# Scaling attention probabilities ahead of the next maxima, and a last output tile by halves, in a one-core decoder layer

## Chip, cores and metric

The kernel runs on one core of a Trainium2 chip. The metric is device time in microseconds of one execution, taken as the median of several runs. All numbers are float32 on the way in and out.

## What is computed

One layer of a hybrid decoder for 1024 prompt rows and 8 x 8 sample rows: an input projection, sliding-window attention with sinks and a relative bias, a pooling mixer, gates, and a squared-ReLU MLP between RMS norms. The two parts that matter here are the softmax of the attention and the last lines of the layer:

```python
s = einsum(q, k) * HEAD_DIM ** -0.5 + bias
m = maximum(max(s, axis=-1), sink)
p = exp(s - m)
denom = sum(p, axis=-1) + exp(sink - m)
o = einsum((p / denom), v)
...
f = square(relu(rms_norm(h, g_pre_mlp) @ w_mlp_up)) @ w_mlp_down
return h + rms_norm(f, g_post_mlp)
```

## The kernel before

Each engine runs its own list of instructions in order, and semaphores tie the lists together. Every product is made of three TensorE products, of high and low parts of both operands (`products`, `row_products`); ScalarE writes the high part of a result and VectorE the low part.

**Attention.** The work is cut into 17 units: 16 of the prompt (two blocks of 128 queries of two heads each; a unit has four score tiles `x`) and one for all sample rows. All engines walk through the same steps `s` (`for s in range(A_STEPS)`), and in step `s` each does a piece of several units, together with one filler: a third of one tile of the input projection (24 products of 384 or 320 columns), which keeps TensorE working between attention pieces.

- TensorE in step `s`: scores of unit `s` (`score_products`, L1344 to L1346), filler group `s + 1` (L1232 to L1234), values of unit `s - 2` (`weigh_values`, L1386, L1390), and the turning (transposing) of the probabilities of unit `s - 1` (`turn_probs`, L1251), which waits for `p_norm`.
- VectorE in step `s`: maxima of unit `s` (four score tiles plus bias into `pr`, L957, and the statistics L967 to L969, which release `stats`); then the scaling of unit `s - 1`: sum of the exponentials (L973), reciprocal (L974), a fold of the two halves of the window (L978), and four multiplications (L983), the last of which releases `p_norm`; then the filler's low part (L891), in every third step the low part of the next weights (L845), the low part of the output of unit `s - 2` (L993), and the masked second copy `pt` of the turned probabilities of unit `s - 1` (L1004).
- ScalarE in step `s`: exponentials of unit `s` (L636, L640), which wait for `stats`; the filler's copy (L580 or L573); every third step the high part of the next weights (L543); the high part of the output of unit `s - 2` (L653); and the first copy `pt` of the turned probabilities of unit `s - 1` (L660).
- GpSimd does the pooling (L469 to L498) from the time the first pooling columns come out of the fillers, around unit 8.

The order on VectorE, where `u` is set twice per step, is

```python
u = s
...
dve.tensor_scalar(stat[:, NM, u % 4, :], ...).then_inc(stats, 1)
u = s - 1
if 0 <= u < A_UNITS:
    dve.wait_ge(expd, u + 1)
...
    one.then_inc(p_norm, 1)
n, c = filler(s + 1)
in_group(n, c)
```

**The end.** The MLP's down products go tile by tile over nine row tiles (`ORDER`). For each tile of the last block TensorE makes 24 products of 512 columns into two banks (`down_tile`, L1469), VectorE adds the 128x1024 result to `acc` (`gather`, L1118), ScalarE squares it with a running sum and takes a root (`y_root`, L828, L833), VectorE multiplies by the gain (`scaled`, L1190), takes the reciprocal and combines with the residual `hb` (`finish`, L1200, L1204), and SyncE stores the 512 KB tile (L394).

Of the kernel before, what the change touches and what calls it, by code (L numbers as in the profile page):

```python
# [8 lines left out]
D = 1024  # L9
# [4 lines left out]
P = 128  # L14
# [5 lines left out]
WIN = 128  # L20
# [12 lines left out]
RT = NBLK + 1  # L33
KXW = WIN + T_DEC
FB = 4
NFB = DFF // (FB * P)
# [18 lines left out]
LAST = NFB - 1  # L55
# [66 lines left out]
def build(nc, I, O):  # L122
# [3 lines left out]
    with ctx:  # L126
# [101 lines left out]
        def sem(name):  # L228
            return ctx.enter_context(nc.semaphore(name))
# [26 lines left out]
        hb_in = [sem(f"hb_in{i}") for i in range(RT)]  # L256
        folds = sem("fold_set")
        f_sq, f_hi, f_lo = sem("f_sq"), sem("f_hi"), sem("f_lo")
        y_fold, y_sq, y_sd, y_rs, y_g, y_r = (sem("y_" + n) for n in ("fold", "sq", "sd", "rs", "scaled", "ready"))
        y_out, moved_out, rows_out, state_out = (sem(n) for n in ("y_out", "moved_out", "rows_out", "state_out"))  # L260
        block = ctx.enter_context(nc.Block())
# [43 lines left out]
        def down_done(blk, p):  # L305

            return blk * PER + (G_M + UPS + p + 1)
# [11 lines left out]
        def down_pair(p):  # L319
            return slice(4 + 2 * (p % 2), 6 + 2 * (p % 2))  # L320
# [39 lines left out]
        @block.sync  # L360
        def _(sp):
            def unit(n, s):
                sp.dma_start(raw[:, s, :], I["weights"][n]).then_inc(raw_in[s], 16)

            def x_load(r):
                if r < NBLK:
                    sp.dma_start(xrow[:, r, :], I["x_prompt"][0, r * P:(r + 1) * P, :]).then_inc(x_in[r], 16)
                else:
                    sp.dma_start(xrow_s[:, :], I["x_sample"].rearrange("b t n -> (b t) n")).then_inc(x_in[r], 16)

            x_load(0)
# [18 lines left out]
            for i, p in enumerate(Y_SEQ):  # L390
# [6 lines left out]
            sp.wait_ge(y_out, 16 * RT)  # L397


        @block.gpsimd  # L400
# [137 lines left out]
        def _(act):  # L538
# [297 lines left out]
            for p in Y_SEQ:  # L836
                y_root(p)


        @block.vector  # L840
        def _(dve):
# [102 lines left out]
            in_group(*filler(0))  # L944
            lo(U_Q + 2)
            for s in range(A_STEPS):
                u = s
                if u < A_UNITS:
                    if u == 0:
# [17 lines left out]
                    chained(dve.tensor_tensor(v4(MM), v4(MX), sk, ALU.max))  # L967
                    dve.tensor_tensor(v4(DD), sk, v4(MM), ALU.subtract)
                    dve.tensor_scalar(stat[:, NM, u % 4, :], stat[:, MM, u % 4, :], -SCALE, None, ALU.mult).then_inc(stats, 1)  # L969
                u = s - 1  # L970
                if 0 <= u < A_UNITS:
                    dve.wait_ge(expd, u + 1)
                    chained(dve.tensor_tensor(stat[:, RR, u % 4, :], stat[:, LL, u % 4, :], stat[:, ES, u % 4, :], ALU.add))  # L973
                    chained(dve.reciprocal(stat[:, RR, u % 4, :], stat[:, RR, u % 4, :]))  # L974
                    if u < A_UNITS - 1:
                        both = slice(1, 4, 2) if u % 4 == 0 else slice(0, 4)
                        p_ = pr[:, u % 2, both, WIN:]
                        dve.tensor_tensor(p_, p_, pr[:, u % 2, both, 0:WIN], ALU.add).then_inc(p_one, 1)  # L978
                        dve.wait_ge(p_one, u + 1)
                    for x in range(4):  # L980
                        k0, kw = keys(u, x) if u == A_UNITS - 1 else (WIN, WIN)
                        p_ = pr[:, u % 2, x, k0:k0 + kw]
                        one = dve.tensor_scalar(p_, p_, stat[:, RR, u % 4, x:x + 1], None, ALU.mult)  # L983
                    one.then_inc(p_norm, 1)
                n, c = filler(s + 1)
                in_group(n, c)
                if c == 0:
# [220 lines left out]
            for p in range(DOWNS):  # L1208
                gather(LAST, p)
                if ORDER[p] < NBLK:  # L1210
                    scaled(p)
                    finish(p)
                if p == 4:
                    scaled(3)
                    finish(3)


        @block.tensor
        def _(pe):
# [5 lines left out]
                if q >= 0:  # L1225
                    pe.wait_ge(freed[FREED[q][0]], FREED[q][1])

            def products(out, terms, inc):

                last = len(terms) - 1  # L1230
                for i, ((wh, wl), (rh, rl)) in enumerate(terms):
                    pe.matmul(out, wh, rh, start=(i == 0), stop=False)  # L1232
                    pe.matmul(out, wh, rl, start=False, stop=False)  # L1233
                    mm = pe.matmul(out, wl, rh, start=False, stop=(i == last))  # L1234
                if inc:
                    mm.then_inc(done, 1)

            def wtile(n, k):
                h, l = slot(n)
# [353 lines left out]
            for p in range(DOWNS):  # L1593
                down_tile(0, p)

            def mlp_block(blk):
# [4 lines left out]
                for p in range(DOWNS):  # L1601
                    down_tile(blk, p)
                    if is_block(blk, LAST) and p == 4:
                        pe.wait_ge(freed["D"], D0 + RT * LAST + 4)
                        pe.wait_ge(freed["A"], A0 + UPS * NFB)
                        sample_sum(ps[:, 0:2, :], acc_s, y_fold)

            with pe.Fori(1, LAST) as blk:
                mlp_block(blk)
            mlp_block(LAST)  # L1610


def bucket_onehot():
# [89 lines left out]
```

## Time and profile before

| | |
|---|---|
| median of 3 runs | 1375.38 us (1374.37 to 1376.09) |
| the profiled execution | 1376.3 us, its span 1374.6 us |
| TensorE products busy | 1349.2 us, 98% of the span |
| VectorE busy | 511.4 us, 37% |
| ScalarE busy | 430.6 us, 31% |
| GpSimd busy | 95.3 us, 7% |
| TensorE idle for `pr` in the attention stage | 5.1 us in 6 pauses |
| mean granted TensorE clock | 0.998 |

The span runs from the first to the last instruction of the core; the execution's own time is 1.7 us longer. A busy share is an average over stages: the attention stage lies between 76 and about 200 us, and the last tile's work between 1361.8 and 1374.6 us.

### The profile page before, as it was taken

Reading aid. Unit: us, or ns where it says so; the run is one execution under the profiler, and the core shown is the slowest. Engines: PE = TensorE matmul, PEld = TensorE weight load, DVE = VectorE, ACT = ScalarE, POOL = GpSimd, SP = SyncE. Lnnn points to the kernel's source line nnn. Section 1 sums busy time; section 2 is a strip of 40 time slices with the busy share of each in tenths; the row PEclk is TensorE's granted clock in tenths of the full one; section 3 lists DMA queues with packets and bytes.
Section 4 is the critical chain, followed back from the end, with each engine's and each line's share of the span. In section 5 each row is a group of like instructions: output and inputs, shape, how many; then the busy total and the mean of one; then the engine's idle time right before and its main releaser. Section 6 shows DMA issues by size and latency. Waiting matters only on the chain.

```text
span 1374.6 us, 18849 instructions
## 1 busy us (share of the span) xinstructions
PE 1349.2 (98%) x7667; PEld 1240.8 (90%) x7667; DVE 511.4 (37%) x879; ACT 430.6 (31%) x821; POOL 95.3 (7%) x148
## 2 busy tenths in 40 slices
PE   6999999999999999999999999999999999999997
PEld 6888889999999998889899899898898998998986
DVE  5468752322222256452323223223132232232256
ACT  5445543211111144354125034042051250340432
POOL 3001583000000001000000000000000000000010
PEclk9999999999999999999999999999999999999999
DMA  9110001111111136220202003012021020030152
GB/s 306 45 36 27 22 32 36 39 39 47 46 47 47 46 101 215 98 77 31 77 15 83 26 15 107 0 46 76 0 76 46 14 80 28 15 107 0 47 186 90
DMA packets 24510, 84.96 MB, mean 62 GB/s; under 512 B 3058, under 2 KB 4232, under 8 KB 24431
## 3 DMA queue, kind: packets, MB, share of 16 engines
q1 hardware_dynamic: 19207, 65.84, 14.3%
q0 software_dynamic: 5248, 18.34, 3.9%
q8 instruction: 41, 0.67, 0.2%
q14 instruction: 14, 0.11, 0.0%
HBM read 74.88 MB, written 10.38 MB: 62 GB/s over the span
## 4 chain that ended last, share of the span: by engine, by line
PE 92%; DVE 3%; ACT 3%; issue 1%; DMA 1%; SPq 0%; DVEq 0%; ACTq 0%
PE ps L1469 32%; PE ps L1232 18%; PE ps L1233 18%; PE ps L1234 18%; PE ps L1477 3%; PE ps L1251 2%; ACT pr L640 1%; DVE pr L957 1%; DMA raw<-in_weights 1%; PE ps L1443 1%; ACT pt L660 0%; DVE pt L1004 0%; PE ps L1546 0%; ACT wr L543 0%; DVE pr L983 0%
## 5 line engine op out<-in xcount | busy, mean ns | idle before, releaser
L1232 PE MATMUL ps<-xn,wr 128*128 128x384 f32 (+1 forms) x1344 | 444.1, 330 | 2.1 <-issue 1.5
L1233 PE MATMUL ps<-xn,wr 128*128 128x384 f32 (+1 forms) x1344 | 441.2, 328 | 0.0
L1234 PE MATMUL ps<-xn,wr 128*128 128x384 f32 (+1 forms) x1344 | 440.9, 328 | 0.0
L1469 PE MATMUL ps<-dn,ff 128*128 128x512 f32 x1536 | 351.6, 389 | 0.0
L1469 PEld LDWEIGHTS ps<-dn,ff 128*128 128x128 f32 x1536 | 287.9, 188 | 60.6 <-DVE acc L1118 0.8
L1232 PEld LDWEIGHTS ps<-xn,wr 128*128 128x128 f32 x1344 | 254.1, 189 | 5.9 <-issue 3.2
L1233 PEld LDWEIGHTS ps<-xn,wr 128*128 128x128 f32 x1344 | 254.0, 189 | 0.3
L1234 PEld LDWEIGHTS ps<-xn,wr 128*128 128x128 f32 x1344 | 253.9, 189 | 0.0
L738 ACT ACTIVATE fa<-ps 128x384 f32<-128x384 f32 (+1 forms) x96 | 45.5, 474 | 496.3 <-PE ps L1234 493.2
L1098 DVE TENSOR_TENSOR ff<-fa,ff 128x384 fp32r<-128x384 f32 (+1 forms) x96 | 49.4, 514 | 252.3 <-ACT ff L742 252.3
L1118 DVE TENSOR_TENSOR acc<-acc,ps 128x1024 f32<-128x1024 f32 x56 | 68.4, 1221 | 195.3 <-PE ps L1469 195.3
L845 DVE TENSOR_TENSOR wr<-raw,wr 128x1024 fp32r<-128x1024 f32 x37 | 45.3, 1225 | 141.8 <-ACT wr L543 141.8
L1469 PE MATMUL ps<-wo,xn 128*128 128x512 f32 x336 | 77.7, 390 | 0.0
L1469 PEld LDWEIGHTS ps<-wo,xn 128*128 128x128 f32 x336 | 63.0, 188 | 13.4
L531 POOL DMA_DIRECT2D hb<-residual_rows x9 | 4.8, 553 | 701.5 <-PE ps L1234 701.5
L669 ACT ACTIVATE sga<-ps,vec 128x384 f32<-128x384 f32 (+1 forms) x24 | 13.5, 564 | 116.6 <-PE ps L1234 116.6
L740 ACT ACTIVATE fa<-fa 128x384 f32<-128x384 f32 (+1 forms) x96 | 48.8, 508 | 3.1
L742 ACT ACTIVATE ff<-fa 128x384 fp32r<-128x384 f32 (+1 forms) x96 | 48.8, 508 | 3.0
L543 ACT ACTIVATE wr<-raw 128x1024 fp32r<-128x1024 f32 x37 | 39.0, 1053 | 31.4 <-PE ps L1234 27.6
L1107 DVE TENSOR_TENSOR dn<-raw,dn 128x1024 fp32r<-128x1024 f32 x28 | 34.3, 1226 | 10.9 <-ACT dn L748 10.9
L1107 DVE TENSOR_TENSOR wr<-raw,wr 128x1024 fp32r<-128x1024 f32 x28 | 33.8, 1224 | 11.2 <-ACT wr L748 11.2
L669 ACT ACTIVATE sgp<-ps,vec 128x384 f32<-128x384 f32 (+1 forms) x24 | 13.5, 564 | 73.6 <-PE ps L1234 73.6
(224 smaller groups left out, 1295.1 us busy)
## 6 DMA issues: line engine op xcount, KB each, us to landing
raw<-in_weights SPq DMA_DIRECT2D x106, 512.0 KB, 3.5
xrow<-in_x_prompt SPq DMA_DIRECT2D x8, 512.0 KB, 11.0
xr<-in_x_prompt POOLq DMA_DIRECT2D x8, 512.0 KB, 6.1
residual_rows<-h POOLq DMA_DIRECT2D x8, 512.0 KB, 3.0
hb<-residual_rows POOLq DMA_DIRECT2D x8, 512.0 KB, 9.3
out_y_prompt<-hb SPq DMA_DIRECT2D x8, 512.0 KB, 2.7
g<-in_vectors POOLq DMA_DIRECT2D x3, 512.0 KB, 4.5
bias_rev<-bias_by_distance POOLq DMA_DIRECT2D x1, 1024.0 KB, 10.9
```

The source lines that it names most:

```text
L738: act.activation(f, ps[:, i % 4, 0:w], ACT.Relu).then_inc(freed["A"], 1)
L740: act.activation(f, f, ACT.Square).then_inc(f_sq, 1)
L742: act.activation(ff[:, j, cs(c)], f, ACT.Copy).then_inc(f_hi, 1)
L845: dve.tensor_tensor(lo_, raw[:, n % 2, :], hi_.bitcast(f32), ALU.subtract).then_inc(w_lo, 1)
L1098: one = dve.tensor_tensor(ff[:, j, LO + c0:LO + c0 + n], fa[i % 2][:, 0:n], ff[:, j, c0:c0 + n].bitcast(f32), ALU.subtract)
L1107: dve.tensor_tensor(dst[:, 1, :], raw[:, x % 2, :], dst[:, 0, :].bitcast(f32), ALU.subtract).then_inc(w_lo, 1)
L1118: dve.tensor_tensor(a, a, src, ALU.add).then_inc(freed["D"], 1)
L1232: pe.matmul(out, wh, rh, start=(i == 0), stop=False)
L1233: pe.matmul(out, wh, rl, start=False, stop=False)
L1234: mm = pe.matmul(out, wl, rh, start=False, stop=(i == last))
L1469: mm = [pe.matmul(out[:, half, :], s, m[:, half * 512:(half + 1) * 512], start=start, stop=stop) for half in range(2)]
L1477: mm = pe.matmul(out[:, half, :], both, moving[part][:, half * 512:(half + 1) * 512], start=first and part == 0, stop=last and part == 1)
```

## The change

In the attention loop VectorE's two blocks trade places: in step `s` it now scales unit `s - 1` first and takes the maxima of unit `s` behind that. The lines themselves are the same.

```diff
             for s in range(A_STEPS):
+                u = s - 1
+                if 0 <= u < A_UNITS:
+                    dve.wait_ge(expd, u + 1)
+                    chained(dve.tensor_tensor(stat[:, RR, u % 4, :], stat[:, LL, u % 4, :], stat[:, ES, u % 4, :], ALU.add))
+                    chained(dve.reciprocal(stat[:, RR, u % 4, :], stat[:, RR, u % 4, :]))
+                    if u < A_UNITS - 1:
+                        both = slice(1, 4, 2) if u % 4 == 0 else slice(0, 4)
+                        p_ = pr[:, u % 2, both, WIN:]
+                        dve.tensor_tensor(p_, p_, pr[:, u % 2, both, 0:WIN], ALU.add).then_inc(p_one, 1)
+                        dve.wait_ge(p_one, u + 1)
+                    for x in range(4):
...
+                    one.then_inc(p_norm, 1)
                 u = s
                 if u < A_UNITS:
...
-                u = s - 1
-                if 0 <= u < A_UNITS:
-                    dve.wait_ge(expd, u + 1)
...
-                    one.then_inc(p_norm, 1)
                 n, c = filler(s + 1)
```

The last output tile (row tile 7) goes by halves of 512 columns: TensorE finishes the left half (12 products) before the right half, and VectorE, ScalarE and the stores follow by halves. The left half is stored by SyncE, the right half by ScalarE's own queue.

```diff
+            n = DOWNS - 1
+            pe.wait_ge(freed["D"], D0 + RT * LAST + n - 1)
+            for half in range(2):
+                cols = slice(half * 512, half * 512 + 512)
+                products(ps[:, down_pair(n).start + half, :],
+                         [(f_rows(k, ORDER[n]), (dn[:, k, 0, cols], dn[:, k, 1, cols])) for k in range(FB)], half == 1,
+                         None if half else y_half)
...
+            for half, (ready, freeing) in enumerate(((y_half, y_part), (done, freed["D"]))):
...
+                dve.tensor_tensor(a, a, ps[:, down_pair(n).start + half, :], ALU.add).then_inc(freeing, 1)
...
+                dve.tensor_tensor(fg[:, n % 2, cols], a, g3[:, cols], ALU.mult).then_inc(y_g, 1)
...
+            for half, ready in enumerate((y_early, y_r)):
+                cols = slice(half * 512, half * 512 + 512)
+                dve.scalar_tensor_tensor(out=hb[:, r, cols], in0=fg[:, n % 2, cols], scalar=rstat[:, 1, r:r + 1],
+                                         in1=hb[:, r, cols], op0=ALU.mult, op1=ALU.add).then_inc(ready, 1)
...
+            act.wait_ge(y_part, 1)
+            act.activation(ysq[:, 0:512], acc[:, r, 0:512], ACT.Square, accum_out=rstat[:, 0, r:r + 1]).then_inc(y_sq, 1)
+            act.wait_ge(y_sq, n + 1)
+            act.activation(rstat[:, 2, r:r + 1], rstat[:, 0, r:r + 1], ACT.Identity, bias=eps, scale=1.0 / D).then_inc(y_sq, 1)
+            act.wait_ge(freed["D"], D0 + RT * NFB)
+            act.activation(ysq[:, 512:], acc[:, r, 512:], ACT.Square, accum_out=rstat[:, 3, r:r + 1]).then_inc(y_sq, 1)
...
+            act.dma_start(O["y_prompt"][0, r * P:(r + 1) * P, 512:], hb[:, r, 512:]).then_inc(y_out, 16)
```

How this moves instructions on VectorE in one step of the attention loop, in the order of before (`pr` are scores and probabilities, `stat` the statistics, ISA is the maxima's instruction with its read-out; the names in brackets are the semaphores waited for):

```order
L1004 TENSOR_TENSOR pt<-pt,earlier 128x512 [waits consts,pt_a,pv,pt_t]
L957 ISA pr,stat<-ps,bias 128x256 [waits pt_t,qk]
...
L967 TENSOR_TENSOR stat<-stat,sink 128x4 [waits s_free]
L968 TENSOR_TENSOR stat<-sink,stat 128x4 [waits dvs]
L969 TENSOR_SCALAR stat<-stat 128x4
L973 TENSOR_TENSOR stat<-stat 128x4 [waits expd]
L974 RECIPROCAL stat<-stat 128x4 [waits dvs]
L978 TENSOR_TENSOR pr<-pr 128x4x128 [waits dvs]
L983 TENSOR_SCALAR pr<-pr,stat 128x128 [waits p_one]
L983 TENSOR_SCALAR pr<-pr,stat 128x128 x3
L891 SCALAR_TENSOR_TENSOR qo<-ps,vec,qo 128x384 [waits in_hi]
```

Before, the maxima follow the `pt` product of the step ahead, and the scaling stands between the statistics and the filler. The same place on VectorE in the order of the change, with the line numbers of the changed kernel:

```order
L1020 TENSOR_TENSOR pt<-pt,earlier 128x512 [waits consts,pt_a,pv,pt_t]
L966 TENSOR_TENSOR stat<-stat 128x4 [waits expd]
L967 RECIPROCAL stat<-stat 128x4 [waits dvs]
L971 TENSOR_TENSOR pr<-pr 128x4x128 [waits dvs]
L976 TENSOR_SCALAR pr<-pr,stat 128x128 [waits p_one]
L976 TENSOR_SCALAR pr<-pr,stat 128x128 x3
L988 ISA pr,stat<-ps,bias 128x256 [waits pt_t,qk]
...
L998 TENSOR_TENSOR stat<-stat,sink 128x4 [waits s_free]
L999 TENSOR_TENSOR stat<-sink,stat 128x4 [waits dvs]
L1000 TENSOR_SCALAR stat<-stat 128x4
L907 SCALAR_TENSOR_TENSOR qo<-ps,vec,qo 128x384 [waits in_hi]
```

The scaling now stands between the `pt` product and the maxima, and the statistics are followed at once by the filler. ScalarE's and TensorE's orders in this stage are the same as before.

The end of VectorE's list before, for the last tile:

```order
L1204 SCALAR_TENSOR_TENSOR hb<-fg,rstat,hb 128x1024 [waits hb_in6,y_scaled,y_rs]
L1118 TENSOR_TENSOR acc<-acc,ps 128x1024 [waits group_done]
L1190 TENSOR_TENSOR fg<-acc,g_110 128x1024 [waits freed_by_vector]
L1200 RECIPROCAL rstat<-rstat 128x1 [waits y_sd]
L1204 SCALAR_TENSOR_TENSOR hb<-fg,rstat,hb 128x1024 [waits hb_in7,y_scaled,y_rs]
```

And with the change:

```order
L1220 SCALAR_TENSOR_TENSOR hb<-fg,rstat,hb 128x1024 [waits hb_in6,y_scaled,y_rs]
L1238 TENSOR_TENSOR acc<-acc,ps 128x512 [waits y_half_done]
L1240 TENSOR_TENSOR fg<-acc,g_110 128x512 [waits y_half_gathered]
L1238 TENSOR_TENSOR acc<-acc,ps 128x512 [waits group_done]
L1240 TENSOR_TENSOR fg<-acc,g_110 128x512 [waits freed_by_vector]
L1242 RECIPROCAL rstat<-rstat 128x1 [waits y_sd]
L1248 SCALAR_TENSOR_TENSOR hb<-fg,rstat,hb 128x512 [waits hb_in7,y_scaled,y_rs]
L1248 SCALAR_TENSOR_TENSOR hb<-fg,rstat,hb 128x512
```

Add, gain and combination of the last tile have become two instructions each, of half the columns.

## Rows read from the trace of the kernel before

**Rows 1.** Waits in 76 to 200 us, then in 200 to 1374 us: total, times, longest.
```profile
PE ps L1251 <- DVE pr L983: 5.1, 6, 1.3
ACT pt L660 <- PE ps L1251: 1.2, 4, 0.5
...
PE ps L1469 <- DVE rstat L1069: 0.4, 1, 0.4
```

**Rows 2.** Timeline of ScalarE: start, duration, instruction, and idle time before it.
```profile
90.60 0.20 ACT L636 ACTIVATE stat<-stat 128x4 f32<-128x4 f32 x1 [2.78 <-DVE stat L969]
...
94.36 0.58 ACT L660 ACTIVATE pt<-ps 128x512 f32<-128x512 f32 x1
98.27 0.20 ACT L636 ACTIVATE stat<-stat 128x4 f32<-128x4 f32 x1 [3.33 <-DVE stat L969]
...
187.17 0.21 ACT L636 ACTIVATE stat<-stat 128x4 f32<-128x4 f32 x1 [2.97 <-DVE stat L969]
```

**Rows 3.** Timeline of VectorE: one scaling, then the next `pt` product and maxima.
```profile
90.47 0.15 DVE L973 TENSOR_TENSOR stat<-stat 128x4 f32<-128x4 f32 x1
...
90.87 0.69 DVE L978 TENSOR_TENSOR pr<-pr 128x512 f32<-128x512 f32 x1
91.60 0.87 DVE L983 TENSOR_SCALAR pr<-pr,stat 128x128 f32<-128x128 f32 x4
...
95.70 0.68 DVE L1004 TENSOR_TENSOR pt<-pt,earlier 128x512 f32<-128x512 f32 x1
96.30 0.42 DVE L957 CUSTOM_DVE_ANT_0 pr<-ps,bias 128x256 f32<-128x256 f32 x1
```

**Rows 4.** VectorE's groups by line, 76 to 206 us: busy us, mean ns, idle before.
```profile
L983 DVE TENSOR_SCALAR pr<-pr,stat 128x128 f32<-128x128 f32 (+1 forms) x68 | 15.9, 297 | 0.6
L1004 DVE TENSOR_TENSOR pt<-pt,earlier 128x512 f32<-128x512 f32 x16 | 13.0, 815 | 2.2 <-ACT pt L660 2.2
L978 DVE TENSOR_TENSOR pr<-pr 128x512 f32<-128x512 f32 (+1 forms) x16 | 10.7, 668 | 0.6
...
L973 DVE TENSOR_TENSOR stat<-stat 128x4 f32<-128x4 f32 x17 | 3.1, 183 | 0.0
L974 DVE RECIPROCAL stat<-stat 128x4 f32<-128x4 f32 x17 | 3.0, 178 | 0.6
```

**Rows 5.** Timeline of TensorE: the turnings of two units in a row.
```profile
106.43 0.66 PE L1251 MATMUL ps<-ident,pr 128*128 128x128 f32 x4
...
113.31 0.66 PE L1251 MATMUL ps<-ident,pr 128*128 128x128 f32 x4
```

**Rows 6.** Timelines of ScalarE, VectorE and TensorE: the last two units.
```profile
190.29 0.60 ACT L660 ACTIVATE pt<-ps 128x512 f32<-128x512 f32 x1 [0.51 <-PE ps L1251]
...
192.44 0.92 DVE L983 TENSOR_SCALAR pr<-pr,stat 128x136 f32<-128x136 f32 x4
...
195.37 1.09 PE L1251 MATMUL ps<-ident,pr 128*128 128x128 f32 x8
```

**Rows 7.** Timeline of the last tile; landing times of the `y_prompt` and `y_sample` stores.
```profile
1367.24 1.22 DVE L1118 TENSOR_TENSOR acc<-acc,ps 128x1024 f32<-128x1024 f32 x1 [1.19 <-PE ps L1469]
1368.49 1.06 ACT L828 ACTIVATE ysq<-acc 128x1024 f32<-128x1024 f32 x1 [3.96 <-DVE acc L1118]
...
1370.20 1.28 DVE L1204 SCALAR_TENSOR_TENSOR hb<-fg,rstat,hb 128x1024 f32<-128x1024 f32 x1
...
DMA to landing us min/median/max: 2.7/2.7/6.7
DMA to landing us min/median/max: 2.9/2.9/2.9
```

**Rows 8.** Stretches: busy and count of PE, PEld, DVE, ACT, POOL; clock; DMA, GB/s.
```profile
180.00:184.00 4.00, 2.72 (x56) 1.97 (x54) 3.14 (x11) 3.30 (x12) 2.83 (x3) 1.00 0.07 24
200.50:204.50 4.00, 4.00 (x66) 3.29 (x66) 0.00 (x0) 0.63 (x2) 3.67 (x5) 1.00 0.00 0
205.00:208.60 3.60, 3.60 (x16) 3.60 (x15) 0.29 (x1) 0.00 (x0) 3.36 (x4) 0.53 0.00 0
```

More of the change, by code:

```diff
@@ L389, in _ @@
                     unit(pair * 2 + s, s)
-            for i, p in enumerate(Y_SEQ):
+            for i, p in enumerate(Y_SEQ[:-1]):
                 r = ORDER[p]
@@ L396, in _ @@
                     sp.dma_start(O["y_sample"].rearrange("b t n -> (b t) n"), hb[0:SROWS, r, :]).then_inc(y_out, 16)
-            sp.wait_ge(y_out, 16 * RT)
+            r = ORDER[-1]
+            sp.wait_ge(y_early, 1)
+            sp.dma_start(O["y_prompt"][0, r * P:(r + 1) * P, 0:512], hb[:, r, 0:512]).then_inc(y_out, 16)
+            sp.wait_ge(y_out, 16 * (RT + 1))
         @block.gpsimd
@@ L834, in y_root @@
                     .then_inc(y_sd, 1)
-            for p in Y_SEQ:
+            for p in Y_SEQ[:-1]:
                 y_root(p)
+            r, n = ORDER[-1], RT - 1
+            act.wait_ge(y_part, 1)
[4 more added lines that the diff above has]
+            act.activation(ysq[:, 512:], acc[:, r, 512:], ACT.Square, accum_out=rstat[:, 3, r:r + 1]).then_inc(y_sq, 1)
+            act.wait_ge(y_sq, n + 3)
+            act.activation(rstat[:, 1, r:r + 1], rstat[:, 3, r:r + 1], ACT.Sqrt, bias=rstat[:, 2, r:r + 1], scale=1.0 / D)\
+                .then_inc(y_sd, 1)
+            act.wait_ge(y_r, RT)
+            act.dma_start(O["y_prompt"][0, r * P:(r + 1) * P, 512:], hb[:, r, 512:]).then_inc(y_out, 16)
         @block.vector
@@ L946, in _ @@
             for s in range(A_STEPS):
+                u = s - 1
[9 more added lines that the diff above has]
+                    for x in range(4):
+                        k0, kw = keys(u, x) if u == A_UNITS - 1 else (WIN, WIN)
+                        p_ = pr[:, u % 2, x, k0:k0 + kw]
+                        one = dve.tensor_scalar(p_, p_, stat[:, RR, u % 4, x:x + 1], None, ALU.mult)
+                    one.then_inc(p_norm, 1)
                 u = s
@@ L969, in _ @@
                     dve.tensor_scalar(stat[:, NM, u % 4, :], stat[:, MM, u % 4, :], -SCALE, None, ALU.mult).then_inc(stats, 1)
-                u = s - 1
-                if 0 <= u < A_UNITS:
-                    dve.wait_ge(expd, u + 1)
[L973 to L983, printed above, removed]
-                    one.then_inc(p_norm, 1)
                 n, c = filler(s + 1)
@@ L1207, in _ @@
             dve.wait_ge(g_bc[2], 16)
-            for p in range(DOWNS):
+            for p in range(DOWNS - 1):
                 gather(LAST, p)
@@ L1215, in _ @@
                     finish(3)
+            r, n = ORDER[-1], RT - 1
+            for half, (ready, freeing) in enumerate(((y_half, y_part), (done, freed["D"]))):
+                cols = slice(half * 512, half * 512 + 512)
+                dve.wait_ge(ready, 1 if half == 0 else down_done(LAST, n))
+                a, before_it = acc[:, r, cols], D0 + RT * LAST + n
+                dve.tensor_tensor(a, a, ps[:, down_pair(n).start + half, :], ALU.add).then_inc(freeing, 1)
+                dve.wait_ge(freeing, 1 if half == 0 else before_it + 1)
+                dve.tensor_tensor(fg[:, n % 2, cols], a, g3[:, cols], ALU.mult).then_inc(y_g, 1)
+            dve.wait_ge(y_sd, n + 1)
+            dve.reciprocal(rstat[:, 1, r:r + 1], rstat[:, 1, r:r + 1]).then_inc(y_rs, 1)
+            dve.wait_ge(y_rs, n + 1)
+            dve.wait_ge(y_g, n + 2)
+            dve.wait_ge(hb_in[r], 16)
+            for half, ready in enumerate((y_early, y_r)):
+                cols = slice(half * 512, half * 512 + 512)
+                dve.scalar_tensor_tensor(out=hb[:, r, cols], in0=fg[:, n % 2, cols], scalar=rstat[:, 1, r:r + 1],
+                                         in1=hb[:, r, cols], op0=ALU.mult, op1=ALU.add).then_inc(ready, 1)
         @block.tensor
@@ L1226, in bank_free, with products @@
                     pe.wait_ge(freed[FREED[q][0]], FREED[q][1])
-            def products(out, terms, inc):
+            def products(out, terms, inc, part=None):
                 last = len(terms) - 1
@@ L1236, in products @@
                     mm.then_inc(done, 1)
+                elif part is not None:
+                    mm.then_inc(part, 1)
             def wtile(n, k):
@@ L1594, in _, with mlp_block @@
                 down_tile(0, p)
-            def mlp_block(blk):
+            def mlp_block(blk, downs):
                 for j, c in MAIN:
@@ L1600, in mlp_block @@
                     up_group(blk, j, c)
-                for p in range(DOWNS):
+                for p in range(downs):
                     down_tile(blk, p)
@@ L1608, in _ @@
             with pe.Fori(1, LAST) as blk:
-                mlp_block(blk)
-            mlp_block(LAST)
+                mlp_block(blk, DOWNS)
+            mlp_block(LAST, DOWNS - 1)
+            n = DOWNS - 1
+            pe.wait_ge(freed["D"], D0 + RT * LAST + n - 1)
+            for half in range(2):
+                cols = slice(half * 512, half * 512 + 512)
+                products(ps[:, down_pair(n).start + half, :],
+                         [(f_rows(k, ORDER[n]), (dn[:, k, 0, cols], dn[:, k, 1, cols])) for k in range(FB)], half == 1,
+                         None if half else y_half)
 def bucket_onehot():
```

1 line of the change is left out of this document (added).

## The prediction

> **What bounds the kernel now.** I read the waits first, then the timeline of the attention stage engine by engine, then the grouped rows and the tail. TensorE is the engine that work queues for almost everywhere, so a change counts where TensorE waits or where it ends. The waits [rows 1] show 5.1 us of TensorE idle in 6 pauses in the attention stage (76 to 200 us), all for the scaled probabilities (`pr`, L983), and 0.4 us in all from 200 us to the end. So whatever the attention stage loses is made good nowhere behind it, and the most that the attention part could win is 5.1 us.
>
> What paces the stage is a ring through ScalarE and VectorE. ScalarE [rows 2] begins the exponentials of unit 2 at 90.60 and then does, in its fixed order, the filler's copy, a weight split, the high half of the output, and at 94.36 the copy of the turned probabilities `pt` of unit 1. VectorE [rows 3] multiplies that copy at 95.70, starts the maxima of unit 3 at 96.30, and the exponentials of unit 3 begin at 98.27 [rows 2]. One round is 98.27 - 90.60 = 7.67 us; from unit 2 to unit 16, which starts at 187.17 [rows 2], the mean round is 96.57 / 14 = 6.90 us. TensorE needs 113.31 - 106.43 = 6.88 us from one turning of probabilities to the next [rows 5]. Ring and TensorE go at the same pace, and there is no slack in either. The scaling stands outside the ring: that of unit 1 ran from 90.47 to 92.47 [rows 3], beside ScalarE's work on unit 2, and was done 1.9 us before the copy at 94.36 that VectorE's next product waits for.
>
> **The attention part: the scaling moves into the ring.** After the change VectorE does, behind the `pt` product, first the scaling and then the maxima. At 95.70 the `pt` product takes 0.68 and the maxima begin at once, at 96.30 [rows 3]: no idle time there in which the scaling could run. What ran beside the exponentials now delays maxima, statistics and exponentials, and through ScalarE's fixed order the next `pt` copy and `pt` product, so each round grows by a whole scaling. In exchange VectorE idles while ScalarE does the exponentials. Nothing is added: the same instructions, one order changed.
>
> How long is a scaling? The four groups of L973, L974, L978 and L983 hold 3.1 + 3.0 + 10.7 + 15.9 = 32.7 us for 17 units [rows 4]. Unit 16 is in the ring's last turn either way; its share is 0.92 [rows 6] + 0.18 + 0.18 (the means [rows 4]), so 31.4 remain for 16 units. Unit 1 shows the gaps between the four: 2.00 from start to end against 0.15 + 0.18 + 0.69 + 0.87 = 1.89 busy, less 0.08 by which the next instruction starts early (95.70 + 0.68 against 96.30 [rows 3]), so 0.03 each, 0.5 in all. That makes **31.9 us**, all on the path, since none of the 16 rounds has slack.
>
> What comes off again: in the ring of before, ScalarE waited for TensorE's turning 1.2 us in 4 places [rows 1]. Now turning follows the scaling while ScalarE is a maxima and an exponential away, so these waits go; 0.51 of them belongs to unit 15 [rows 6] and is counted below, and of the other 0.7 I take 0.5. So the exponentials of unit 16 start 31.4 us later.
>
> At the end of the stage some is won back. Before, unit 15's scaling came after unit 16's statistics, so TensorE still had a turning, a filler and the values to do, and turned unit 16 at 195.37 [rows 6] although its scaling had ended at 192.44 + 0.92 = 193.36. Now unit 15 is turned before unit 16's exponentials begin, TensorE is ready, and ScalarE's 0.51 of waiting at 190.29 is gone: the turning follows at 193.36 - 0.51 = 192.85 in the same count, **2.5 us** earlier. The stage ends 31.4 - 2.5 = **28.9 us later**. TensorE waits about 2 us longer in each round (the 5.1 of before are inside this sum).
>
> The bounds of this term come from GpSimd, whose pooling runs beside VectorE from unit 8 on and stretches its rows. From below: a scaling as at unit 1 (1.92) twelve times and one with the 0.27 shorter fold of `u % 4 == 0` four times makes 29.6, so 2.3 less; and if the `pt` products lose their stretch too (mean 0.815 [rows 4] against 0.68 [rows 3], times 16), another 2.2 less. From above: as much stretch again, 4.5 more. I take the rows as they stand, since GpSimd has the same work to do beside VectorE's same instructions.
>
> What would the longer idle do to the clock? While TensorE worked only 2.72 of 4 us and waited out 1.28 us, its granted clock stayed 1.00, the 2.4 GHz level [rows 8]; it fell once, to 0.53 in 205.0 to 208.6, after 4 us of small products (32 columns) with no pause at all [rows 8]. I forecast 1.00 through the stage: a stretch of 3.6 us at half the clock loses 1.7 us, and 2 us of idle in each round cover even that. The Trainium skill (TensorE: Matmul & The Clock Gate, § HAM oscillation — how this bites in real kernels) says that a kernel which makes TensorE wait again and again between bursts is throttled anew before each burst. By that rule the sum would be the second rival's below; by the row it is nothing. The trace agrees with the rule only in that a thin stretch was followed by the lower level.
>
> **The tail.** Before, the last product ended at 1367.24 and then came one after another: add 1.22, square 1.06 and its sum, root, reciprocal, and the last combination at 1370.20 for 1.28 [rows 7], then the store, 2.7 us to landing in the median [rows 7]. Now the first half's add, gain and square are done while TensorE makes the second half; 12 products per half, the same 24 in all, so TensorE loses nothing. Left behind the product are a half add (0.69, as the 128x512 row of L978 [rows 3]) instead of 1.22, and a half square (0.58, as the 128x512 copy [rows 2]) instead of 1.06: 0.53 + 0.48 = **1.0 us**. The two combinations of half a row take together what one took; the added Identity runs ahead of the second half. The store is now 256 KB on ScalarE's own queue beside 256 KB on SyncE's, issued some 0.6 earlier. The one store of 256 KB in the trace landed after 2.9 us [rows 7], against 2.7 for 512 KB, so I take no saving there. ScalarE's queue has carried no transfer before, and no row shows one. Bounds for the tail: 2.3 won, if the landing shrinks with the bytes (half of 2.7), to 3.0 lost, if the store lands as late as the slowest of `y` did, after 6.7 [rows 7]; I stay at 2.7, the median.
>
> **The sum.** The profiled execution took 1376.3 us, 0.9 above the median of the three runs (1375.38). Attention +28.9, tail -1.0, together +27.9: 1404.2 for such an execution, **1403.3** as a median; I forecast 1403 us, 2.0% slower.
>
> **Rivals.** *The pauses go, as the order on paper suggests: faster.* The probabilities are scaled right after the `pt` product, TensorE finds them ready, the 5.1 us fall to nothing, and with the tail the time is 1375.4 - 5.1 - 1.0 = 1369.3. This needs a ring with at least 2 us to spare per round, so that the scaling hides behind a waiting VectorE. For it speaks that VectorE idles in each round, for instance before the filler's part. Against it: that idle lies beside the exponentials, not between `pt` product and maxima, and is not where the scaling is put; the ring of 6.90 has to become shorter than TensorE's 6.88 plus the pauses, and it becomes 8.9. Chance 0.04.
>
> *The clock falls.* If all 24 filler products of each round ran at half the clock, some 4.2 us more per step, TensorE would need 11.1 us, more than the ring: 16 x (11.1 - 6.9) = 67, so some 1441 us. It decides once the low level lasts longer in a round than the 2 us of idle cover, about 4 us. Against it: [rows 8], and that TensorE at half the clock pauses less. Chance 0.04.
>
> *Nothing moves.* If the scaling only trades its place inside time in which VectorE would have waited for ScalarE anyway, the pauses stay and only the tail is won: 1374.4. It would need an idle VectorE ahead of the maxima, of which [rows 3] show none. Chance 0.02.
>
> **How the numbers follow.** Forecast 0.90. The bounds of the attention term (-4.5, +4.5) and of the tail (-1.3, +4.0) reach from 1397.5 to 1411.8; both tail and stage at one end together is unlikely, and the range is 1397 to 1411. About 0.15 lies outside: the rivals' 0.10 and as much as may miss the bounds. Some 0.2%, 2.8 us, is what a measurement of this kernel can tell from no change; by the cases it is faster 0.04, the same 0.02, slower 0.94.
>
> **What would show it.** Right: a round of 8.5 to 9.5 us from exponentials to exponentials; TensorE's waits for `pr` grow from 5.1 to some 30 to 35 us, in nearly all 16 rounds; VectorE's wait for ScalarE's exponentials (filler, split or `qo`) grows likewise; exponentials of unit 16 near 218; behind the stage the same times shifted by some 29; from last product to the store's issue some 1 us less. Wrong: rounds that stay near 7 us (the ring isn't closed as I read it), a granted clock of half in the stage, or a stage that ends at about 200.

## The result, and the profile after

The changed kernel takes **1404.3 us** (1403.68 to 1405.21, 4 runs) against 1374.88 for the kernel before on the same chip (1373.76 to 1376.09, 4 runs): a ratio of 1.0211, 95% interval 1.0199 to 1.0223. The forecast was 1403 in 1397 to 1411. The profiled spans are 1403.5 and 1374.6 us, 28.9 apart. Lines have moved by the added code: in the changed kernel ScalarE's exponentials are L640 and L644, its `pt` copy L664, its output high half L657; VectorE's scaling is L966 to L976, its maxima L988, statistics L998 to L1000, `pt` product L1020; TensorE turns at L1287, scores at L1380, values at L1422.

First the ring. ScalarE's timeline after, with the columns of [rows 2]: a `pt` copy, the exponentials of two units in a row, the last unit's exponentials, and the last output copy, which ends the attention stage.

```profile
97.05 0.58 ACT L664 ACTIVATE pt<-ps 128x512 f32<-128x512 f32 x1
102.88 0.20 ACT L640 ACTIVATE stat<-stat 128x4 f32<-128x4 f32 x1 [5.25 <-DVE stat L1000]
...
110.63 0.21 ACT L640 ACTIVATE stat<-stat 128x4 f32<-128x4 f32 x1 [4.37 <-DVE stat L1000]
...
219.53 0.20 ACT L640 ACTIVATE stat<-stat 128x4 f32<-128x4 f32 x1 [5.52 <-DVE stat L1000]
...
234.74 0.38 ACT L657 ACTIVATE qo<-ps 128x256 fp32r<-128x256 f32 x1 [3.28 <-PE ps L1436]
```

One round is 110.63 - 102.88 = 7.75 us. Before, the same round ran from 98.27 [rows 2] to the first row below and took 5.84: a difference of 1.91, which is one scaling. Unit 16's exponentials start at 219.53 instead of 187.17 [rows 2]. The second row below is the one of before that answers to the last row here:

```profile
104.11 0.20 ACT L636 ACTIVATE stat<-stat 128x4 f32<-128x4 f32 x1 [2.45 <-DVE stat L969]
...
204.45 0.39 ACT L653 ACTIVATE qo<-ps 128x256 fp32r<-128x256 f32 x1 [3.20 <-PE ps L1400]
```

So the attention stage ends 234.74 - 204.45 = 30.3 us later, and the tail must give 1.4 back. The stage also began 0.9 us earlier in this execution: the first unit's exponentials start at 78.91, against 79.79 before. From there to the last output copy it takes 155.83 us instead of 124.66, 31.2 more.

Where in the round the time goes is on VectorE. Its timeline after, around one `pt` product early in the stage and around one late, while GpSimd works beside:

```profile
98.39 0.68 DVE L1020 TENSOR_TENSOR pt<-pt,earlier 128x512 f32<-128x512 f32 x1
98.99 0.15 DVE L966 TENSOR_TENSOR stat<-stat 128x4 f32<-128x4 f32 x1
...
100.12 0.88 DVE L976 TENSOR_SCALAR pr<-pr,stat 128x128 f32<-128x128 f32 x4
100.91 0.42 DVE L988 CUSTOM_DVE_ANT_0 pr<-ps,bias 128x256 f32<-128x256 f32 x1
...
214.76 0.79 DVE L966 TENSOR_TENSOR stat<-stat 128x4 f32<-128x4 f32 x1
215.59 0.18 DVE L967 RECIPROCAL stat<-stat 128x4 f32<-128x4 f32 x1
215.80 1.19 DVE L971 TENSOR_TENSOR pr<-pr 128x512 f32<-128x512 f32 x1
217.02 1.14 DVE L976 TENSOR_SCALAR pr<-pr,stat 128x128 f32<-128x128 f32 x4
```

Before, the maxima followed the `pt` product at once, at 96.30 after 95.70 [rows 3]. Now a scaling of 2.0 us stands between them (98.99 to 101.00), and late in the stage one of 3.4 (214.76 to 218.16). I cut each of the 15 rounds from unit 1's exponentials to unit 16's at the same four points in both timelines and summed:

| part of the round, 15 rounds | before | after | change |
|---|---|---|---|
| exponentials start to `pt` copy end | 55.9 | 54.7 | -1.3 |
| `pt` copy end to `pt` product start | 5.4 | 5.5 | +0.2 |
| `pt` product | 12.3 | 11.8 | -0.5 |
| `pt` product end to maxima start | -1.2 | 33.8 | **+35.0** |
| maxima start to next exponentials | 30.0 | 28.2 | -1.8 |
| sum | 102.4 | 134.0 | +31.6 |

With the round of unit 0 (+1.65) the 16 rounds cost +33.2 us. Everything new stands in the one gap into which the diff puts the scaling.

TensorE's side: the waits in 76 to 240 us, with the columns of [rows 1]; two rows of ScalarE and VectorE stand ahead, and those of `PE` are TensorE's.

```profile
ACT stat L640 <- DVE stat L1000: 85.1, 17, 6.4
DVE qo L1009 <- ACT qo L657: 25.1, 7, 7.6
...
PE ps L1287 <- DVE pr L976: 11.7, 11, 1.9
...
PE ps L1380 <- DVE stat L988: 5.3, 10, 0.7
PE ps L1422 <- DVE pt L1020: 4.1, 4, 1.3
```

With 0.9 and 0.7 in two smaller rows TensorE waits 22.7 us where it waited 5.1 [rows 1]: 17.6 more. The rest hides as busy time. The first part of the profile's page says

```profile
PE 1361.8 (97%) x7667; PEld 1251.5 (89%) x7667; DVE 515.1 (37%) x882; ACT 430.6 (31%) x824; POOL 95.4 (7%) x148
```

that is 12.6 us more than before for the same 7667 instructions, and 17.6 + 12.6 - 1.4 (tail) = 28.8, the span's difference. The reason is in the windows after (columns of [rows 8]):

```profile
92.00:106.00 14.00, 11.06 (x77) 9.66 (x76) 8.01 (x32) 7.46 (x25) 0.00 (x0) 0.83 0.11 37
...
179.00:195.00 16.00, 14.37 (x93) 13.02 (x94) 9.62 (x36) 6.66 (x25) 5.97 (x7) 0.79 0.02 7
...
181.50:184.00 2.50, 2.50 (x16) 2.28 (x17) 0.24 (x2) 2.21 (x10) 0.00 (x0) 0.50 0.00 0
```

In 92 to 106 us TensorE works 11.06 of 14 us at a mean granted clock of 0.83; in 181.5 to 184 it is at 0.50, the 1.2 GHz level. Before, both long windows were at 1.00; the first of them read

```profile
92.00:106.00 14.00, 13.83 (x121) 12.13 (x121) 11.72 (x46) 8.22 (x30) 0.00 (x0) 1.00 0.11 39
```

Whether this costs time or only fills a wait that the ring makes anyway is the first question for the runs.

The tail after: add, square, root, combination and the last store's issue, then the landing of the two half stores.

```profile
1397.58 0.68 DVE L1238 TENSOR_TENSOR acc<-acc,ps 128x512 f32<-128x512 f32 x1
...
1398.29 0.63 ACT L848 ACTIVATE ysq<-acc 128x512 f32<-128x512 f32 x1 [0.27 <-DVE acc L1238]
...
1399.05 0.29 ACT L850 ACTIVATE rstat<-rstat 128x1 f32<-128x1 f32 x1
...
1399.57 1.41 DVE L1248 SCALAR_TENSOR_TENSOR hb<-fg,rstat,hb 128x512 f32<-128x512 f32 x2
...
1401.02 0.38 ACTq L853 DMA_DIRECT2D out_y_prompt<-hb  x1
```
```profile
out_y_prompt<-hb SPq DMA_DIRECT2D x1, 256.0 KB, 2.0
out_y_prompt<-hb ACTq DMA_DIRECT2D x1, 256.0 KB, 2.1
```

From the last add to the span's end it is 1403.5 - 1397.58 = 5.92 us, against 1374.6 - 1367.24 = 7.36 [rows 7]: 1.44 won.

### The profile page after: what moved, and what is told of

It is laid out like the page before. It is cut to its first block, busy times and chain, and to the rows that moved or that the text cites. A ratio compares the mean times of both kernels' runs of the same rounds, so it can differ in the third digit from the quotient of the medians.

```text
span 1403.5 us, 18856 instructions
## 1 busy us (share of the span) xinstructions
PE 1361.8 (97%) x7667; PEld 1251.5 (89%) x7667; DVE 515.1 (37%) x882; ACT 430.6 (31%) x824; POOL 95.4 (7%) x148
## 4 chain that ended last, share of the span: by engine, by line
PE 87%; DVE 6%; ACT 5%; issue 1%; DMA 1%; SPq 0%; DVEq 0%; ACTq 0%
PE ps L1505 31%; PE ps L1266 17%; PE ps L1267 17%; PE ps L1268 17%; PE ps L1513 3%; ACT pr L644 2%; DVE pr L988 2%; PE ps L1287 1%; DVE pr L976 1%; DVE pt L1020 1%; DVE pr L971 1%; DMA raw<-in_weights 1%; PE ps L1479 1%; ACT wr L547 0%; ACT pt L664 0%
## 5 line engine op out<-in xcount | busy, mean ns | idle before, releaser
L1505 PE MATMUL ps<-dn,ff 128*128 128x512 f32 x1512 | 346.3, 389 | 0.0
L1505 PEld LDWEIGHTS ps<-dn,ff 128*128 128x128 f32 x1512 | 283.4, 188 | 59.8 <-DVE acc L1134 0.8
L1266 PEld LDWEIGHTS ps<-xn,wr 128*128 128x128 f32 x1344 | 257.3, 191 | 6.5 <-issue 4.2
L1267 PEld LDWEIGHTS ps<-xn,wr 128*128 128x128 f32 x1344 | 257.5, 192 | 0.3
L1268 PEld LDWEIGHTS ps<-xn,wr 128*128 128x128 f32 x1344 | 257.0, 191 | 0.0
L1123 DVE TENSOR_TENSOR wr<-raw,wr 128x1024 fp32r<-128x1024 f32 x28 | 33.8, 1224 | 11.3 <-ACT wr L752 11.3
## 6 DMA issues: line engine op xcount, KB each, us to landing
xrow<-in_x_prompt SPq DMA_DIRECT2D x8, 512.0 KB, 10.4
bias_rev<-bias_by_distance POOLq DMA_DIRECT2D x1, 1024.0 KB, 10.6
```

What stands on the lines that cost most here:

```text
L1123: dve.tensor_tensor(dst[:, 1, :], raw[:, x % 2, :], dst[:, 0, :].bitcast(f32), ALU.subtract).then_inc(w_lo, 1)
L1505: mm = [pe.matmul(out[:, half, :], s, m[:, half * 512:(half + 1) * 512], start=start, stop=stop) for half in range(2)]
```

## The experiments

The theory under test, called the ring theory: VectorE's scaling stands in a chain through ScalarE and VectorE that has no slack, so its length is added to every round. Its rivals: TensorE's lower clock makes the time; VectorE's work costs time wherever it stands; the scaling delays the scores or the turning directly.

**e1, the attention part alone:** the kernel before with only VectorE's scaling moved (the two hunks of the diff in VectorE's attention loop; the tail as before).

> The attention part alone, the last tile as before. Ring theory (the scaling now lies in the ring VectorE - ScalarE, each round grows by a scaling): all of the loss and none of the tail's gain, so the changed kernel's 1404.3 plus 1.4 (from last product to the end 7.36 us before, 5.98 after): 1405.7, 1404.5 to 1407. Rival, that part of the loss is the tail's (a store on a new queue, one more semaphore chain): below 1404.

Measured: 1407.8 us (1407.2 to 1408.2), ratio 1.0233 (1.0217 to 1.0248) to a kernel before at 1375.6. Exponentials from 80.5 to 221.1, 140.6 us as in the changed kernel. The attention part alone costs 32.2 us, and the time lies 0.8 beyond the expected range. In its profiled execution the stage is as long as in the changed kernel (155.80 us from the first exponentials to the last output copy), but starts 1.56 us later (80.47 against 78.91). So what e1 has over the changed kernel beside the tail lies, in the traces, ahead of the stage and not in it.

**e2, the tail alone:** the changed kernel with the scaling back behind the maxima.

> The last tile by halves alone, attention as before. Both parts are independent if e1 and e2 add up: 1374.9 - 1.4 = 1373.5, 1372.5 to 1374.5. If the tail's halves cost something while the stage hides it, 1375 or more.

Measured: 1374.5 us (1372.3 to 1375.0), ratio 0.9993 (0.9984 to 1.0002): 1.1 us won, at the upper end of the expected range, and not more than these runs can tell from nothing. TensorE waits for `pr` 4.9 us in 5 places, much as before, and the stage is 124.60 us long. Together e1 and e2 make +31.1 us, the whole change +29.4; the difference is within their intervals, and nothing here shows that one part changes what the other costs.

**e3, ScalarE's order:** the changed kernel, but ScalarE copies unit `s - 2`'s output and unit `s - 1`'s `pt` ahead of the exponentials of unit `s` instead of behind them, so that the `pt` copy no longer waits through exponentials, filler and split.

```diff
+                u = s - 2
+                if 0 <= u < A_UNITS:
+                    act.wait_ge(pv, u + 1)
...
+                    act.activation(pt[:, 0:4, :], ps[:, 4, :].rearrange("p (b n) -> p b n", n=P), ACT.Copy).then_inc(pt_a, 1)
...
-                u = s - 2
-                if 0 <= u < A_UNITS:
-                    act.wait_ge(pv, u + 1)
...
-                    act.activation(pt[:, 0:4, :], ps[:, 4, :].rearrange("p (b n) -> p b n", n=P), ACT.Copy).then_inc(pt_a, 1)
```

> The changed kernel with one more edit: ScalarE does the output's high half and the pt copy of a step ahead of the exponentials, not behind the filler. Ring theory: where the filler needs VectorE's low part (units 0 to 7) VectorE still reaches the pt product only behind exponentials and filler, so nothing is won; from unit 8 on, in the five rounds without a weight split, output half and pt product run beside the exponentials and the ring falls from some 8.9 to some 6.5 us: 5 x 2.3 = 11.5 us less, 1393, 1389 to 1398. Rival clock theory (the stage is longer because TensorE was granted 0.79 to 0.93 there): TensorE has the same idle or more in the first half, so the time stays at 1402 to 1406. Rival, TensorE's scores wait for later maxima: their order is not touched, 1404.

Measured: 1396.7 us (1395.7 to 1398.0), ratio 1.0155 (1.014 to 1.0171); exponentials from 77.4 to 210.6, 133.2 us. No instruction was added or removed, and 8.3 of the 29.4 us are gone (each kernel against the kernel before on its own chip: 1396.7 - 1375.6 = 21.1, 1404.3 - 1374.9 = 29.4): in the expected range, out of the rivals'. Up to unit 16's exponentials 7.4 us are won, in four rounds from unit 9 on and none before; five such rounds and 11.5 us were expected. What is left of the chain is VectorE's filler part, weights' low part and output low half, which stand ahead of the `pt` product and wait for ScalarE.

**e4, the ring opened:** e3, and VectorE does the filler's and the weights' low part at the end of the step, behind the `pt` product, one filler later.

```diff
-                n, c = filler(s + 1)
-                in_group(n, c)
...
+                if s:
+                    n, c = filler(s)
+                    in_group(n, c)
```

> e3 and one more edit: VectorE does the filler's low part and the weights' low part at the end of a step, one filler later, behind the pt product. Ring theory: the ring is now exponentials 2.1, scaling 2.0, maxima 1.85 and some 0.3 of hand-overs, 6.2 us, shorter than TensorE's mean step of 6.65: TensorE paces the stage, the 5.1 us of pauses of before mostly go as well, and with the tail's 1.4 it takes 1368.5, 1367 to 1374. If the order scaling before maxima is itself what costs (scores held back by later maxima, a lower clock), it stays above 1385.

Measured: 1383.2 us (1382.2 to 1383.6), ratio 1.0054 (1.004 to 1.0067). Much of the loss is gone, but the forecast of this run fell: 14.7 too low. TensorE's waits in 76 to 205 us show why:

```profile
PE ps L1271 <- DVE qo L907: 10.6, 8, 1.7
PE ps L1385 <- DVE stat L988: 1.8, 3, 0.7
PE ps L1292 <- DVE pr L976: 1.4, 2, 1.2
```

The wait for `pr` is nearly gone, and a new one stands in its place: the first product of a filler (L1271) waits for VectorE's low part (L907). Fillers alternate between two PSUM banks, and VectorE's low part gives a bank back; done at the step's end, it comes after TensorE wants the bank. Without it the time would be some 1383.2 - 10.6 = 1372.6.

**e5, TensorE kept busy:** the changed kernel with six throwaway products of 128x512 per step on TensorE in 15 steps, three on either side of the turning, into an unused bank (added work).

```diff
+                spare = 3 if 2 <= s <= A_UNITS else 0
+                for _ in range(spare):
+                    pe.matmul(ps[:, 7, :], xn[:, 0, 0, 0:P], xn[:, 0, 1, 0:512], start=True, stop=True)
...
+                for _ in range(spare):
+                    pe.matmul(ps[:, 7, :], xn[:, 0, 0, 0:P], xn[:, 0, 1, 0:512], start=True, stop=True)
```

> The changed kernel with six throwaway products of 512 columns per step on TensorE (three before and three behind the turning, 6 x 0.23 = 1.4 us, into a bank that nobody reads), to keep TensorE busy where it waits. Ring theory: TensorE has some 2 us of idle per round, so the time stays within 1402 to 1407 while the granted clock in the stage rises towards 1.00. Clock theory: the clock rises and the stage gets shorter, by up to the 12.6 us that TensorE's busy time grew from before to the change: 1392 to 1399.

Measured: 1406.2 us (1405.6 to 1407.0), ratio 1.0223 (1.0206 to 1.024), the same as the changed kernel within the intervals; exponentials from 76.9 to 217.7, 140.8 us. The windows of e5:

```profile
92.00:106.00 14.00, 13.21 (x104) 11.43 (x102) 8.71 (x28) 7.06 (x23) 0.00 (x0) 1.00 0.11 37
...
179.00:195.00 16.00, 15.07 (x116) 12.63 (x115) 9.51 (x33) 6.67 (x25) 6.97 (x8) 1.00 0.00 1
```

The granted clock is 1.00 in these windows and in all seven others between 92 and 215 us, and nothing is won. That the added products eat up what the clock gives back is no way out: each of the 16 rounds is within 0.05 us as long as in the changed kernel, and TensorE still waits 10.4 us in the stage. The clock theory falls: the lower clock in the changed kernel filled waits and made none.

**e6, a delay in the ring:** the kernel before, its order untouched, with two throwaway copies of 128x512 on VectorE between `pt` product and maxima in 16 steps (added work).

```diff
+                for _ in range(2 if 1 <= s < A_UNITS else 0):
+                    chained(dve.tensor_copy(ps[:, 7, :], xn[:, 0, 0, 0:512].bitcast(f32)))
```

> The kernel before with two throwaway copies of 128x512 on VectorE per step, in the place where the change put the scaling (between the pt product and the maxima); scaling and maxima keep their order. They take some 0.4 to 0.7 us each, so 0.8 to 1.4 in each of 16 rounds. Ring theory: the place costs, whatever stands there: nearly all of 16 x 0.8 to 1.4 is lost, 1387 to 1397. If the order of scaling and maxima were the cause, two copies would cost little: 1375 to 1379.

Measured: 1397.6 us (1395.2 to 1398.0), ratio 1.0155 (1.0138 to 1.0172): 21.7 us more, 0.6 above the range. Its VectorE group (columns of [rows 4]) and TensorE's wait:

```profile
L948 DVE COPY ps<-xn 128x512 f32<-128x512 f32 x32 | 22.1, 690 | 0.6
```
```profile
PE ps L1253 <- DVE pr L985: 16.8, 12, 2.6
```

22.1 us of copies cost 21.7, and six of the rounds 1 to 7 grow by 1.45 or 1.46 us each, two copies with their gaps: what is put into this place costs its full length, scaling or not.

**e7, the same delay beside the exponentials:** the kernel before with the same 32 copies behind the scaling.

> The kernel before with the same two copies on VectorE per step, behind the scaling, beside ScalarE's exponentials, outside the ring. Ring theory: 0.8 us of idle lies there in units 0 to 7 and 1 us and more later, so most of it is covered: 1375 to 1379. If simply more work on VectorE costs, the same as in e6.

Measured: 1380.6 us (1379.2 to 1383.6), ratio 1.0036 (1.0021 to 1.005): 4.7 us more, 1.6 above the range, and far from e6's 21.7. TensorE's waits for `pr` rise to

```profile
PE ps L1253 <- DVE pr L983: 8.4, 10, 2.2
```

So VectorE's place there has slack, but not 1.4 us (two copies) in every round. Its trace shows which rounds pay: six of the rounds 1 to 7 grow by 0.14 to 0.62 us, 2.8 in all, and two late ones (units 12 and 14) by 1.09 and 1.36.

**e8, the bank given back early:** e4, with VectorE's filler and weights' low parts directly behind the maxima and statistics.

```diff
                    dve.tensor_scalar(stat[:, NM, u % 4, :], ...).then_inc(stats, 1)
+                if s:
+                    n, c = filler(s)
+                    in_group(n, c)
+                    if c == 0:
+                        lo(n + 1)
...
-                if s:
-                    n, c = filler(s)
-                    in_group(n, c)
-                    if c == 0:
-                        lo(n + 1)
```

> The ring opened as in e4 (the changed VectorE order kept: scaling ahead of the next maxima; ScalarE's output high half and copy of the transposed probabilities ahead of the exponentials), but VectorE's filler low part and the weights' low part stand right behind the maxima and statistics instead of at the step's end. Ring theory with the bank wait as e4's only loss: e4's 10.6 us of TensorE waiting for a filler's bank go, since VectorE had idled up to 1.7 us at just that place; the product pass paces the stage again, mean round about 6.9, and the time is e4's 1383.2 - 10.6 = 1372.6, in 1369 to 1376: the reordered scaling then costs nothing, whatever its place. Rival (scaling ahead of the maxima costs VectorE's chain from exponentials to exponentials its length in any order, scaling 2.4 + maxima 1.9 + exponentials 2.1 and hand-overs): it stays at 1380 or above, with TensorE waiting for scores' banks or for pr instead.

Measured: 1373.6 us (1369.1 to 1374.2, 11 runs), ratio 0.9976 (0.9967 to 0.9986) to a kernel before at 1376.2, in the range. TensorE's waits in 76 to 205 us, and one VectorE step:

```profile
PE ps L1385 <- DVE stat L988: 1.8, 3, 0.7
PE ps L1292 <- DVE pr L976: 0.6, 2, 0.4
PE ps L1392 <- DVE stat L988: 0.2, 1, 0.2
```
```profile
118.36 0.16 DVE L1000 TENSOR_SCALAR stat<-stat 128x4 f32<-128x4 f32 x1
118.43 0.61 DVE L907 SCALAR_TENSOR_TENSOR qo<-ps,vec,qo 128x384 fp32r<-128x384 f32 x1
118.95 1.22 DVE L861 TENSOR_TENSOR wr<-raw,wr 128x1024 fp32r<-128x1024 f32 x1
120.09 0.42 DVE L1010 TENSOR_TENSOR qo<-ps,qo 128x256 fp32r<-128x256 f32 x1
120.42 0.68 DVE L1021 TENSOR_TENSOR pt<-pt,earlier 128x512 f32<-128x512 f32 x1
```

The bank's wait is gone; all of TensorE's waits in the stage come to 2.6 us against 5.1 before [rows 1], and the scaling still stands ahead of the maxima. The two low parts now stand right behind the statistics, where VectorE in e4 waited for the exponentials (11.3 us in 12 places). The stage takes 122.85 us from the first exponentials to the last output copy, 1.8 less than before.

**e9, the tail alone again,** on e8's chip, so that the two can be compared.

> The same kernel as e2 (the halved tail alone), as a measure beside e8 on one chip: 1374.5, in 1372 to 1375.5, ratio to before 0.998 to 1.000. If e8 is at or below it, the changed VectorE order costs nothing once the ring is opened; if e8 is 5 us or more above it, something in the order still costs.

Measured: 1374.8 us (1372.0 to 1375.4, 11 runs), ratio 0.9989 (0.998 to 0.9998), 1.4 us below the kernel before; its stage takes 124.66 us, as before. e8 is 1.3 us faster still. The two intervals just overlap, but nine of e8's eleven runs lie below ten of e9's eleven, and e8's stage is 1.8 us shorter. So with the ring opened, the scaling ahead of the maxima loses nothing against the old order in its closed ring. Whether it wins or costs anything against the old order in an opened ring stays open: no run has that kernel.

## Why the prediction was right

**The ring.** Right, and it carries the result. Rounds 1 to 7, with no GpSimd beside them, grew by 1.91 to 1.92 us six times and once by 1.29 (a shorter fold, and a ScalarE wait that went): the 1.92 of unit 1's scaling to the hundredth. e6 shows that the place costs what is put into it, e7 that the same work beside the exponentials costs a fifth, and e8 that with the chain opened on both engines (ScalarE's copies ahead of the exponentials, VectorE's low parts behind the statistics) the kernel with the scaling in the same place is no slower than the kernel before. The round was forecast at 8.5 to 9.5 us; the 15 rounds of the table take 8.9 in the mean (7.61 to 10.74).

**The sum of the scalings.** Forecast +31.4 at unit 16's exponentials, measured +33.2. The term that was too small is GpSimd's stretch. The forecast took the rows of before as they stood, "since GpSimd has the same work to do beside VectorE's same instructions". It has, but other instructions now meet. VectorE's groups after, for 76 to 235 us:

```profile
L976 DVE TENSOR_SCALAR pr<-pr,stat 128x128 f32<-128x128 f32 (+1 forms) x68 | 17.7, 332 | 0.6
...
L971 DVE TENSOR_TENSOR pr<-pr 128x512 f32<-128x512 f32 (+1 forms) x16 | 11.9, 741 | 0.6
...
L966 DVE TENSOR_TENSOR stat<-stat 128x4 f32<-128x4 f32 x17 | 5.5, 321 | 0.0
```

These are 1.8, 1.2 and 2.4 us more than in [rows 4]; the sum for L966 is up most, since it is the first to start while GpSimd's instruction runs (0.79 at 214.76, against 0.15 undisturbed, while GpSimd is in two sums from 214.32 to 216.43). The Trainium skill (SBUF — State Buffer, § Who interferes with whom) says that a VectorE instruction with two inputs in SBUF and a GpSimd instruction that reads SBUF exclude each other, the later waiting out the earlier. That sum and the fold of L971 have two such inputs, and their rows fit the rule; L976 multiplies one tile by a factor per row, so the sentence does not cover its 1.8. No run here moved GpSimd's work to test either. Against this 5.4, the maxima and the rest of the round lost 3.4 of theirs (the table's other lines). The upper bound of 4.5 had room for it. A smaller slip stands in the forecast's sum itself: it gave unit 16's sum of exponentials the mean of 0.18, where the trace of before has 0.57 for that one, so 31.0 and not 31.4 belonged to the 16 units.

**What comes back at the end of the stage.** Forecast -2.5. Unit 16's exponentials start 32.4 us later (219.53 against 187.17; the ring began 0.9 earlier in this execution), the stage ends 30.3 later: -2.1. Unit 15 is turned before unit 16's exponentials, as forecast, and ScalarE's 0.51 is gone; but unit 16's scaling now follows a `pt` product of 1.13 us instead of 0.69, beside GpSimd, and that takes 0.4 of it. Stage +28.9 forecast; measured +30.3 at its end, +31.2 from its own start (31.14 in e1). So the stage was forecast 2.3 us too low, and in the profiled executions the earlier start (0.9) and the tail (0.4) hid over half of that: the spans are 28.9 apart where 27.9 was forecast. To that extent the nearness of the number is luck.

**TensorE's waits.** Forecast 30 to 35 us for `pr`; measured 11.7 for `pr` and 22.7 in all. The products took 12.6 us longer at the lower clock, which shows as busy time; with that it is 35.3, about the size that was forecast. But the wait that was named is a third of it: 6.0 us are scores that wait for the maxima and 4.1 values that wait for `pt`, which the forecast didn't name.

**The clock.** This step failed: "I forecast 1.00 through the stage." It was 0.79 to 0.96 in eight of ten windows between 92 and 225 us. [rows 8] showed one stretch with 1.28 us of waiting in 4 that stayed at 1.00, and I took that for every such stretch. A granted clock of half in the stage stood among the forecast's own signs of being wrong; it came (0.50 in 181.5 to 184), and the time was right all the same. The rule that I set aside, of the Trainium skill (TensorE: Matmul & The Clock Gate, § HAM oscillation — how this bites in real kernels), tells of a kernel that waits again and again and is throttled anew each time. That was nearer to the clock that came. But the kernel of that section waits longer than it works between two waits; here TensorE worked 11.06 of 14 us, no recorded wait was longer than 1.9, and the clock fell all the same. It was not the better guide to the time. The rival built on it stood at 1441, and e5, with the clock back at 1.00, is no faster: the ring was slower than TensorE even at the lower clock, so the clock cost nothing here. The forecast had that covering argument too (2 us of idle in each round), and it is what held.

**The tail.** Forecast -1.0, measured -1.4. The half add and half square gave what was forecast: add to square 1.25 to 0.71 (-0.54), square to root 1.18 to 0.76 (-0.42). The two half combinations take 1.41 instead of 1.28 (+0.13). The term that was mis-sized is the store: "I take no saving there". The half stores landed after 2.0 and 2.1 us, against 2.7 for the whole tile [rows 7], 0.6 won. The one row of 256 KB that I took as the price, 2.9, was `y_sample`, which uses half the partitions with rows as long as before; the half of a row on all partitions is another shape.

**The other rivals.** "The pauses go" and "nothing moves" needed an idle VectorE ahead of the maxima, and the table shows there was none. Only e8 came near the first, by another change: 1373.6 against 1369.3, with 2.6 us of pauses left.

## What to carry to other kernels

Before an instruction is moved on an engine that looks idle, follow the chain through all engines that hands one round to the next, and ask whether the new place is inside it: VectorE was 37% busy over the span, though 77% in 76 to 200 us (94.93 of 124), and 2 us put into the wrong gap cost about 2 us sixteen times. In e8 the same order stands in a kernel that is no slower than before, because ScalarE's and VectorE's orders around it were changed too. So an idea and the order around it have to be moved together, and each moved step must be asked what it frees (in e4 a PSUM bank). The start of a stage differs between executions (the first exponentials start at 76.9 to 80.5 us in the eleven traces), so two traces are better compared from the stage's own start. When TensorE's busy time grows with the same instructions, look at the granted clock, and then at what paces the stage before calling the clock the cause.

## What the runs showed of the hardware that was not expected

- TensorE's granted clock fell in a stage in which no recorded wait was longer than 1.9 us; in one window of it TensorE was busy for 79% of the time (11.06 of 14 us, clock 0.83). With six extra products per step (e5) it stayed at 1.00 from 92 to 215 us.
- A 256 KB store of half rows from 128 partitions landed after 2.0 us, a 512 KB store of whole rows after 2.7, and a 256 KB store of whole rows from 64 partitions after 2.9 [rows 7]. ScalarE's queue, unused before, landed its first store in 2.1.
- A VectorE sum of 128x4 elements took 0.15 us alone and 0.79 while a GpSimd instruction ran; four multiplications of 128x128 took 0.88 alone and 1.14 late in the stage.
